# Router moved onto split fp32r products of the residual's own half blocks, the first expert's index taken ahead of the softmax, stores and loads in another order

## The reference

```
h  = RMSNorm(x);  q, k, v, gates = h @ W_in
y  = (sigmoid(gate_A) * (A @ W_branch_A) + sigmoid(gate_B) * (B @ W_branch_B)) @ W_out
x1 = x + y
h2 = RMSNorm(x1) * g_ffn
logits = h2 @ w_router + b_router                 # 32 experts
top 4 of 32, softmax over the four
x  = x1 + sum over the four of gate * expert(h2)  # clamped SwiGLU, 1024 -> 2 x 1024 -> 1024
out = RMSNorm(x)
```

## Time and profile before

| | |
|---|---|
| median of 3 runs | 1560.65 us (1560.32 to 1561.15) |
| profiled execution | 1559.76 us |
| its span, from the first instruction to the last | 1558.0 us |
| mean granted clock of PE | 0.986 |
| PE busy | 1512.6 us, 97% |
| DVE, ACT, POOL busy | 1311.9, 1091.1, 268.3 us |
| output projection starts | 321.92 us |
| last `residual` starts | 369.21 us |
| first gather starts | 385.83 us |
| first expert product | 395.91 us |

### The profile page before, as it was taken

How to read it: one execution, slowest core, us unless ns; L and a number is a source line. 1 busy time by engine, 2 the same in 40 slices (tenths; PEclk the granted TensorE clock), 3 DMA queues, 4 the chain that set the end, 5 groups by cost and what they waited for, 6 DMA issues and landing times.

```text
span 1558.0 us, 21230 instructions
## 1 busy us (share of the span) xinstructions
PE 1512.6 (97%) x7254; PEld 1240.9 (80%) x7287; DVE 1311.9 (84%) x1021; ACT 1091.1 (70%) x1158; POOL 268.3 (17%) x164
## 2 busy tenths in 40 slices
PE   7999999997999999999999999999999999999997
PEld 6888788886788888888888888888888888888884
DVE  4556587656899999999999999999999999999975
ACT  4344587424787777877777787787777778778772
POOL 6302144100001110111100001202120022002211
PEclk9999999998899999999999999999999999999997
DMA  8330001545999999999999999999999999999972
GB/s 299 122 100 36 1 1 55 200 141 181 378 363 391 385 389 385 379 391 379 375 387 386 386 387 381 388 390 385 376 372 391 386 378 394 387 387 380 388 263 113
DMA packets 131102, 477.36 MB, mean 306 GB/s; under 512 B 9720, under 2 KB 10240, under 8 KB 130976
## 3 DMA queue, kind: packets, MB, share of 16 engines
q1 hardware_dynamic: 117536, 434.79, 72.1%
q0 software_dynamic: 9936, 36.44, 9.1%
q10 hardware_dynamic: 3600, 5.73, 1.1%
HBM read 452.81 MB, written 24.12 MB: 306 GB/s over the span
## 4 chain that ended last, share of the span: by engine, by line
PE 93%; DVE 3%; ACT 2%; issue 1%; DMA 0%; ACTq 0%; SPq 0%; DVEq 0%
PE ps L1446 28%; PE ps L1447 28%; PE ps L1448 28%; PE ps L1708 2%; PE ps L1716 2%; PE ps L1735 2%; PE ps L1494 1%; PE ps L1537 1%; DVE pT_lo L1155 1%; PE ps L1538 0%; ACT probs L754 0%; PE ps L1479 0%; DMA xs<-in_x 0%; DVE split L1068 0%; PE ps L1515 0%
## 5 line engine op out<-in xcount | busy, mean ns | idle before, releaser
L1279 DVE TENSOR_TENSOR chunk_lo<-chunk,chunk_hi 128x2048 fp32r<-128x2048 f32 x384 | 859.3, 2285 | 39.0 <-ACT chunk_hi L879 36.0
L879 ACT ACTIVATE chunk_hi<-chunk 128x2048 fp32r<-128x2048 f32 x378 | 722.6, 1914 | 109.2 <-PE ps L1448 108.1
L1446 PE MATMUL ps<-chunk_hi,XT 128*128 128x512 f32 x1024 | 404.8, 395 | 2.0 <-DVE XT L1324 2.0
L1448 PE MATMUL ps<-chunk_hi,XT 128*128 128x512 f32 x1024 | 400.0, 391 | 0.0
L1447 PE MATMUL ps<-chunk_lo,XT 128*128 128x512 f32 x1024 | 399.9, 391 | 0.0
L644 POOL DMA_INDIRECT sum_rows<-y,idx x31 | 116.4, 3755 | 921.7 <-ACT y L985 833.8
L1446 PEld LDWEIGHTS ps<-chunk_hi,XT 128*128 128x128 f32 x1024 | 192.8, 188 | 41.1 <-DVE XT L1324 2.4
L1448 PEld LDWEIGHTS ps<-chunk_hi,XT 128*128 128x128 f32 x1024 | 192.4, 188 | 40.4
L1447 PEld LDWEIGHTS ps<-chunk_lo,XT 128*128 128x128 f32 x1024 | 192.8, 188 | 38.9
L1446 PE MATMUL ps<-chunk_hi,hidT 128*128 128x512 f32 x512 | 200.4, 391 | 0.0
L1448 PE MATMUL ps<-chunk_hi,hidT 128*128 128x512 f32 x512 | 200.1, 391 | 0.0
(11 more groups left out here) (272 smaller groups left out, 1900.7 us busy)
## 6 DMA issues: line engine op xcount, KB each, us to landing
chunk<-in_w_gate_up SPq DMA_DIRECT2D x256, 1024.0 KB, 8.8
chunk<-in_w_down SPq DMA_DIRECT2D x128, 1024.0 KB, 7.1
raw<-in_w_in SPq DMA_DIRECT2D x14, 1024.0 KB, 6.8
xs<-in_x SPq DMA_DIRECT2D x8, 512.0 KB, 5.2
w_out<-in_w_out SPq DMA_DIRECT2D x4, 1024.0 KB, 6.8
raw<-in_w_branch_a SPq DMA_DIRECT2D x2, 1024.0 KB, 6.0
raw<-in_w_branch_b SPq DMA_DIRECT2D x2, 1024.0 KB, 6.9
sum_rows<-xs ACTq DMA_DIRECT2D x4, 512.0 KB, 2.6
```

The costliest lines, as they stand in the source:

```text
L879: a.activation(chunk_hi[hi_slot(c, nxt)][:, :], chunk[c][:, :], ACT.Copy).then_inc(ex_hi, 1)
L1279: v.tensor_tensor(chunk_lo[c][:, :], chunk[c][:, :], chunk_hi[hi_slot(c, nxt, first)][:, :].bitcast(F32), ALU.subtract).then_inc(ex_lo, 1)
L1446: mm(dst, lhsT(0), rhs(0), start=start, stop=False)
L1448: return mm(dst, lhsT(1), rhs(0), start=False, stop=stop)
```

## The change

1. The router takes x1 itself, before the norm. PE turns each half block as soon as it is added (`x1_turn(n)`, four transposes), ACT rounds the result (`x1T_round`), DVE takes the remainder (`x1T_remain`), and `router(n)` makes 12 fp32r products with the router's weights stationary (32 columns) and 128 tokens moving. `g_ffn` is multiplied into the weights beforehand, and they are split once (`wr_hi`, `wr_lo`). The logits come out with experts as rows: ACT copies them (`logits_out`), PE turns them back (`logits_turn`), and `choose` scales by the reciprocal root.
2. Turns, router blocks and quarters of the projection are interleaved by hand on PE.
3. The first index is made of two columns of `feats`, ahead of the softmax, which now runs for all four blocks at once while the gather is under way. The first gates follow in products of their own. `slots(1)` and `slots(2)` move behind `weigh(1)` and `weigh(2)`; with them `index(1)`, `index(2)`, `serve(1)`, `serve(2)`.
4. The first expert's rows are released to ACT after four of the eight transposes, and the first two chunks' products wait for half of `XT` alone.
5. Block 3 of `acc` and of `h2buf` is stored from SP's queue instead of ACT's, in between the loads of chunks 4 and 5 and behind them. Chunks 6 and 7 are loaded after the first gather instead of before it.
6. The last block's mean square is taken by halves (`half_square`). Some semaphores are shared.

```diff
@@ SP
-            sp.wait_ge(wout_ps, 2 * NT)
+            sp.wait_ge(x1_ready, 2 * NT)
+            sp.dma_start(acc[3 * 128:SEQ, :], xs[:, 3, :]).then_inc(rows_stored, 16)
+            load_expert(sp, 4, 0)
+            load_expert(sp, 5, 0)
+            sp.wait_ge(xn2_ready, NT)
+            sp.dma_start(h2buf[3 * 128:SEQ, :], xn2[3]).then_inc(rows_stored, 16)
             sp.dma_start(bd[:, :], b_down[0]).then_inc(bd_in, 16)
-            for c in range(4, 8):
-                load_expert(sp, c, 0)
             sp.wait_ge(scattered, ADDED)
             sp.dma_start(bias_tab[:, :], bias_parts).then_inc(bias_back, 16)
             sp.wait_ge(gathered, 16)
-            for c in range(8, 12):
+            for c in range(6, 12):
                 load_expert(sp, c, 0)
@@ ACT
             act.dma_start(g16[0:8, :], g_mix.rearrange("l (k p) -> (l k) p", p=128)).then_inc(g_mix_in, 16)
+            act.dma_start(g16[8:16, :], g_ffn.rearrange("l (k p) -> (l k) p", p=128)).then_inc(g_mix_in, 16)
...
+            def x1T_round(n):
+
+                act.wait_ge(x1T_ps, n + 1)
+                if n >= 4:
+                    act.wait_ge(logits_ps, n - 3)
+                a.activation(x1T_hi[:, n % 4, :, :], ps[:, n % 2, :].rearrange("p (k n) -> p k n", n=128),
+                             ACT.Copy).then_inc(x1T_top, 1)
+
+            def logits_out(c):
+
+                act.wait_ge(logits_ps, 2 * c + 2)
+                a.activation(lgT[:, c % 2, :], ps[0:E, 2 + c % 2, 0:128], ACT.Copy).then_inc(lgT_out, 1)
...
             act.wait_ge(branch_ps, KD)
             first_split_hi(0)
-            root(3)
-            h2T_half(2)
+            x1T_round(4)
+            logits_out(1)
+            root(2)
...
+            x1T_round(6)
+            half_square(1)
+            act.wait_ge(sq2_done, 6)
+            a.activation(ss[:, 3:4], ss_half[:, 1:2], ACT.Sqrt, bias=ss_half[:, 0:1]).then_inc(rt2_done, 1)
+            x1T_round(7)
+            logits_out(3)
             a.activation(warm[:, :], eps[:, :], ACT.Exp)
-            store_rows(3)
...
+            for c in range(NT):
+                top_exp(c)
...
+            first_split_hi(1)
+            act.wait_ge(idx_first, 1)
+            a.activation(f5[:, 0:2], ps[0:CAP, 5, 440:442], ACT.Copy).then_inc(f2_ready, 1)
...
+            a.activation(idx[:, 0:1], f5[:, 0:1], ACT.Identity, bias=s1[:, 0:1]).then_inc(idx_ready, 1)
...
+            act.wait_ge(xt_first, 1)
+            a.activation(XT[:, 0, 0:4, :].rearrange("p k n -> p (k n)"), ps[:, 6, 0:4 * CAP], ACT.Copy).then_inc(xt_hi, 1)
+            rows_hi(1, 1)
+            first_split_hi(3)
             act.wait_ge(gates_set, 1)
-            first_split_hi(3)
             index(1, slice(1, 2))
             act.wait_ge(gates_set, 2)
-            act.wait_ge(logits_ps, NT)
             index(2, slice(2, 3))
-            rows_hi(1, 0)
-            rows_hi(1, 1)
...
             act.wait_ge(rows_stored, 2 * NT * 16)
             first_split_hi(4)
@@ DVE
+            def x1T_remain(n):
+                dve.wait_ge(x1T_top, n + 1)
+                v.tensor_tensor(x1T_lo[:, n % 4, :, :], ps[:, n % 2, :].rearrange("p (k n) -> p k n", n=128),
+                                x1T_hi[:, n % 4, :, :].bitcast(F32), ALU.subtract).then_inc(x1T_rest, 1)
...
             serve(0)
+            softmax(0, NT)
+            ex_split_lo(0, 1, first=True)
+            ex_split_lo(0, 2, first=True)
+            rows_lo(1, 0)
+            rows_lo(1, 1)
+            ex_split_lo(0, 3, first=True)
+            dve.wait_ge(idx_done, 1)
+            serve(1)
...
@@ PE
+            def x1_turn(n):
+                pe.wait_ge(x1_ready, n + 1)
+                if n >= 2:
+                    pe.wait_ge(x1T_rest, n - 1)
+                for k in range(4):
+                    at = n % 2 * 512 + k * 128
+                    last = t_.transpose(ps[:, n % 2, k * 128:(k + 1) * 128], xs[:, n // 2, at:at + 128], ident[:, :])
+                last.then_inc(x1T_ps, 1)
+
+            def router(n):
+                c = n // 2
+                pe.wait_ge(x1T_rest, n + 1)
+                if n == 0:
+                    pe.wait_ge(wr_rest, 1)
...
+                for k in range(4):
+                    kk = n % 2 * 4 + k
+                    last = mm_split(ps[0:E, 2 + c % 2, 0:128], lambda p: (wr_hi, wr_lo)[p][:, kk, :],
+                                    lambda p: (x1T_hi, x1T_lo)[p][:, n % 4, k, :], start=(kk == 0), stop=(kk == KD - 1))
...
+            def logits_turn(c):
+                pe.wait_ge(lgT_out, c + 1)
+                t_.transpose(ps[:, 2 + c % 2, 128:128 + E], lgT[:, c % 2, :], ident[0:E, 0:E]).then_inc(lg_ps, 1)
...
+            out_part(5, 2)
+            x1_turn(4)
+            logits_turn(1)
+            out_part(5, 3)
+            out_part(6, 0)
+            router(4)
+            out_part(6, 1)
+            x1_turn(5)
+            out_part(6, 2)
+            out_part(6, 3)
+            router(5)
+            out_part(7, 0)
+            logits_turn(2)
+            out_part(7, 1)
+            x1_turn(6)
+            out_part(7, 2)
+            router(6)
+            out_part(7, 3)
             pe.wait_ge(wout_ps, 2 * NT)
             pe.sem_inc(ex_used, 2)
-            h2_transpose(2)
-            router(1)
-            router(2)
-            h2_transpose(3)
-            router(3)
+            x1_turn(7)
+            router(7)
+            logits_turn(3)
...
-            pe.wait_ge(f5_ready, 3)
-            rows_in(1)
-            pe.wait_ge(xt_lo, 2)
...
             for c in range(4):
+                if c % 2 == 0:
+                    pe.wait_ge(xt_lo, c // 2 + 1)
                 if c == 3:
                     pe.wait_ge(bias_back, 16)
                     pe.wait_ge(pick_set, 1)
                     add_bias(0, 0, 0)
                 weigh(c, c, c, XT, 0, c == 0, c == 3).then_inc(ex_used, 1)
+                if c in (1, 2):
+                    slots(c)
+            pe.wait_ge(f5_ready, 3)
```

More of the change, by code:

```diff
@@ L190, in encoder_block @@
         chunk_in = [sem(f"chunk_in{s}") for s in range(NIN)]
-        wo_in = [sem(f"wo_in{s}") for s in range(4)]
+        wo_in = acc_in = x_in
+        X_IN, WO_IN, ACC_IN = 16, 32, 48
         expert_in = [sem(f"expert_in{s}") for s in range(NCH)]
@@ L263, in encoder_block @@
         rows_stored = sem("rows_stored")
-        h2T_ps = sem("h2T_ps")
-        h2T_a = sem("h2T_a")
-        h2T_d = sem("h2T_d")
+        wr_scaled = sem("wr_scaled")
+        x1T_ps = sem("x1T_ps")
+        x1T_top = sem("x1T_top")
+        x1T_rest = sem("x1T_rest")
+        wr_top = sem("wr_top")
+        wr_rest = sem("wr_rest")
+        lgT_out = sem("lgT_out")
+        lg_ps = sem("lg_ps")
+        idx_first = sem("idx_first")
+        f2_ready = sem("f2_ready")
+        gates_known = sem("gates_known")
+        xt_first = sem("xt_first")
         logits_ps = sem("logits_ps")
@@ L306, in encoder_block @@
         sums_ready = sem("sums_ready")
-        acc_in = [sem(f"acc_in{c}") for c in range(NT)]
         gfin_in = sem("gfin_in")
@@ L852, in wo_split_hi @@
             def wo_split_hi(j):
-                act.wait_ge(wo_in[j], 16)
+                act.wait_ge(wo_in[j], WO_IN)
                 a.activation(wo_hi[j][:, :], wo[j][:, :], ACT.Copy).then_inc(wo_hi_done, 1)
@@ L1343, in _ @@
             v.tensor_copy(items_i[:, 0:1], npass[:, :]).then_inc(items_ready, 1)
-            dve.wait_ge(idx_done, 1)
-            serve(1)
-            for c in range(1, 3):
-                ex_split_lo(0, c, first=True)
             dve.wait_ge(idx_done, 2)
             serve(2)
-            ex_split_lo(0, 3, first=True)
-            rows_lo(1, 0)
-            rows_lo(1, 1)
             dve.wait_ge(items_ready, 1)
@@ L1414, in add_up @@
                 c = ENDS[n]
-                dve.wait_ge(acc_in[c], 16)
+                dve.wait_ge(acc_in[c], ACC_IN)
                 dve.wait_ge(sums_ps, n + 1)
@@ L1667, in _ @@
                     out_part(n, j)
-            out_half(4)
-            out_half(5)
-            h2_transpose(0)
-            out_half(6)
-            router(0)
-            h2_transpose(1)
-            out_half(7)
+            out_part(4, 0)
+            x1_turn(0)
+            out_part(4, 1)
+            x1_turn(1)
+            out_part(4, 2)
+            router(0)
+            x1_turn(2)
+            out_part(4, 3)
+            router(1)
+            x1_turn(3)
+            out_part(5, 0)
+            router(2)
+            logits_turn(0)
+            out_part(5, 1)
+            router(3)
+            out_part(5, 2)
[16 more added lines that the diff above has]
+            out_part(7, 3)
             pe.wait_ge(wout_ps, 2 * NT)
             pe.sem_inc(ex_used, 2)
-            h2_transpose(2)
-            router(1)
-            router(2)
-            h2_transpose(3)
-            router(3)
+            x1_turn(7)
+            router(7)
+            logits_turn(3)
             for c in range(NT):
@@ L1736, in add_bias @@
```

(25 more changed lines are left out.)

148 lines of the change are left out of this document (79 added, 69 removed).

## The result

The changed kernel took 1577.26 us (median of 8 executions, 1570.61 to 1599.00); the kernel before, beside it on the same chip, 1561.85 (8 executions, 1560.32 to 1574.88). The ratio is 1.0074, with a 95% interval of 1.0049 to 1.0098: slower, and the median lies above the predicted range. The ratio leaves out the two executions of the changed kernel that took over 1.5% more than its fastest (1595.92 and 1599.00); with them in, the medians stand 1% apart. The profiled execution took 1578.71 us, its span 1577.0, which is 19.0 more than before.

What follows compares the result with a forecast made beforehand. PE bounds the kernel (97% of the span), with DMA as full in the loop. First product 2.0 later plus 5.8 of start stalls gives +7.8, with 0.5 for the clock: profiled 1568.1, median 1569.0, range 1562.5 to 1573.

Steps and rivals of the forecast that it cites:

- Step 1: Projection stage: added transposes, router blocks and waits make it grow by 6.6 to 6.8 us, last product ending at 376.0.
- Steps 2 and 3: Tail and gather: index allows 386.3, but the last h2 store holds the gather to 389.6, landing at 395.5.
- my middle estimate: Landing of the last h2 store, issued at 380.3: about 388.7, from 6.8 for a first load plus queued transfers.
- Steps 4 and 5: Gather landing to first product takes 2.4 us; then stalls at the loop's start cost 5.8 more up to slots(3).
- S': Start of the first expert product in the changed kernel, predicted at 397.9, 2.0 us later than before.
- the sum to `slots(3)`: First product 2.0 us later plus 5.8 at the loop's start: +7.8 us.
- the start stalls: Loop's start: PE idle 2.4 us at product 4 and 3.1 us at slots(3).
- Behind it both run the same loop.: From slots(3), the first instruction both orders share, to the end: loop otherwise adds nothing.
- 0.5 for the clock: Low clock after the second stall at the loop's start: costs 0 to 2.6 us, taken as 0.5.
- `hidden_T(1)`: Next late place in the loop: DVE comes 13.5 after serve(3) starts, PE 12.8 after slots(3); it just holds.
- rival (d): Chunks 6 and 7 behind the gather queue two more MB; hidden_T(1) may wait: up to +3 us, 1572, chance 0.10.
- the share of 1.03: DMA share in one expert of the loop, 388 GB/s: transfers have little to spare, PE delays are not won back.

Runs made afterwards that it cites:

- e12: Changed kernel: chunks 6, 7 before gather, 4, 5 rounded first, later scatter wait, h2 store before loads, logits_turn(1) later, first index earlier; 1564.68 us, ratio 1.0015.
- e6: Changed kernel with the last h2 rows stored from ACT's queue instead of SP's; 1572.04 us, ratio 1.0088.
- e3: Changed kernel with ACT rounding chunks 4 and 5 before index(1) and index(2) instead of behind them; 1572.86 us, ratio 1.0069.
- e5: Kernel before with only chunks 6 and 7 moved behind the first gather; 1568.36 us, ratio 1.0042.
- e2: Changed kernel with chunks 6 and 7 loaded ahead of the gather again; 1572.55 us, ratio 1.0055.
- e1: Changed kernel run once more with no edit; 1571.89 us, ratio 1.0068.
- e4: Changed kernel with chunks 6 and 7 loaded ahead of the gather and chunks 4 and 5 rounded before index(1) and index(2); 1567.56 us, ratio 1.0042.
- e7: Changed kernel with last h2 rows stored from ACT's queue, chunks 6 and 7 ahead of the gather, chunks 4 and 5 rounded first; 1568.04 us, ratio 1.0054.
- e8: Changed kernel: h2 store on ACT's queue, chunks 6, 7 before gather, 4, 5 rounded first, logits_turn(1) later, first index earlier; 1575.02 us, ratio 1.0077.
- e11: Changed kernel: chunks 6, 7 before gather, 4, 5 rounded first, later scatter wait, h2 store ahead of loads on SP's queue; 1565.89 us, ratio 1.0014.
- e9: Changed kernel with the scatter wait moved behind the copy of the slot sums, to the index column write; 1571.41 us, ratio 1.0069.
- e10: Kernel before with the scatter wait moved behind the copy of the slot sums, to the index column write; 1562.53 us, ratio 0.9989.
- e15: e12 with slots(1), slots(2), their indices and chunk 3's rounding back ahead of the gather's wait, chunks 6 and 7 behind the gather; 1569.34 us, ratio 1.0058.

## Why the prediction was wrong

**Step 1, the projection: right.** Its last add starts at 375.70 (predicted 376.0). Router products start 0.06 us apart (0.065 predicted); PE waits 0.83 at `logits_turn(1)` (1.0 predicted). The Trainium skill (TensorE: Matmul & The Clock Gate, LDWEIGHTS) has the load of a stationary operand take its columns divided by 1.2, in ns. The trace agrees in the difference: a load of 32 columns has a mean of 109 ns from start to end, one of 128 columns 188, so 79 for 96 columns, where an estimate by that rule gives 80. The load is hidden as well: the spacing is my bound for the streaming alone (0.057), nothing on top.

**Steps 2 and 3: right.** The gather is released by the store, at 388.84 (389.6). The store took 8.6 us; my middle estimate had been 8.4 from an issue at 380.3. That it fits so well is in part luck: the terms that I named (6.8, 2.6 and 1.3 from 377.3) add up to 388.0 and not to the 388.7 that I wrote. What sets the landing e12 and e6 show: 3.0 us with the loads behind it in its queue, 9.0 us on ACT's queue with two loads issued 3.4 us earlier on SP's (and 0.6 MB more behind these). The Trainium skill (DMA: Bandwidth & Descriptors, Queues, rings and completion order) says that an engine takes turns between queues; a store that gained by its turn would have landed sooner, and here it did not.

**Steps 4 and 5: right in place, wrong in worth.** S' was 397.50 (397.9), the idle at product 4 was 2.25 (2.4), that at `slots(3)` 1.23 (3.1, with part of product 5 at the low clock instead), and the sum to `slots(3)` +7.53 (+7.8). But e3 took 4 us of the start stalls out and the time stayed: behind them the next expert's chunks were late anyway. I had added costs that lie beside each other.

**The step that failed: "Behind it both run the same loop."** It carried the sum from `slots(3)` to the end with nothing added but 0.5 for the clock. They run the same code, not the same loop. The sum had 8.3, the profiled execution has 19.0. The 10.7 between them are 0.95 in the first turn, 8.86 in the next four, 1.16 more at the end (1.66 against the 0.5), less 0.3 up to `slots(3)`.

The large term is the ring, the 8.86 us. Of them 7.3 are landings beyond 13.4 us, and 1.6 the low clock in the fifth turn. I had looked at `hidden_T(1)` for DVE's lateness and found 0.7 us of room, and not at ACT's wait for the scatter ahead of `index`.

The other is the backlog, my rival (d) with its size: I gave it "up to +3" and 0.10. In the kernel before it alone is 6.9 (e5). In the changed kernel it adds only 0.95 to `slots(4)`, since PE comes late by its own stalls. `slots(4)` is 8.48 later than before: 3.19 from the issue (394.89 against 391.70) and 5.29 from the longer way to it (63.24 against 57.95). 2.1 MB at 410 GB/s is 5.1. Without the backlog the stalls would have cost as much (e2), and without the stalls the backlog (e3). I had read the share of 1.03 and written that a delay of PE is not won back; the same row says it of a delay of a transfer.

Without the ring's turns the profiled execution would be at 1569.9, close to the lowest timings (1570.61, 1570.67, 1570.71) and to my 1569.0. That this comes so close is in part luck: the clock took 1.66 where I had 0.5, and the first turn 0.95 where I had nothing. That the higher timings are the ring is shown for profiled executions only (e1, e4, e7, e8, e11).

**What stays open.** Why the scatter lands after 14 to 17 us and not after 11 is not shown: e4, e8 and e11 show it with no chunk late, and e6 does not, with backlog and stalls. Why the ring ends is half seen. In all four profiled executions in which it ended (the changed kernel, e1, e4, e8) its last rest was longer, 23.68, 23.70, 23.71 and 24.95 us instead of 22.09, with the granted clock at or near 0.5 behind `hidden_T`, and the next scatter landed after 9.1 to 11.9. In e7, where it held, 28 rests in a row are 22.06 to 22.10. So one slower turn seems to let the transfers catch up; no run tests it. What made the clock low there and in the last turn is open too.

No version came out below the kernel before. The best by its median, e12_all (1564.68), is 1.0015 times it, which the 0.2% bound does not tell from no change. My reading, which no run isolates: the index is ready earlier, but the projection is longer (its last add starts at 373.63 in e12, 369.21 before) and holds back the chunk loads (issued from 378.28, before from 369.59) that the gather must then share the transfers with.

## What to carry to other kernels

Where a loop shows a DMA share near 1 beside a full PE, count the bytes queued behind a critical transfer as carefully as those ahead of it, and take delays that end at the same later wait as a maximum, not a sum. In such a loop look for rings that pass through a transfer (landing plus a fixed rest) and compare the rest with the turn: here 13.4 us of landing was the edge, and 10.5 to 12.3 were in use in the kernel before. A wait belongs at the write that it protects; moving it took 2.1 us out of the ring, though it did not move the median (e9, e10).

## What the runs showed that I had not expected

- A scatter of 128 rows lands after 9.1 to 13.5 us in quiet turns (6.0 to 7.3 in the last turn) and after 14.1 to 17.3 in others. Nearly all turns of an execution can be quiet (the kernel before), and nearly all late (e7, 1622.16 us; e11, 1592.95 us).
- A 512 KB store takes 3.0 us ahead of two 1 MB loads, 8.6 behind them in their queue, and 9.0 on a queue of its own with them issued 3.4 us earlier.
- A gather takes 6.0 us, 8.5 with two chunk loads issued 5 us ahead of it (e15), 9.5 with four (e12).
